# A macaron trunk on one core: the first modulation and the first products in two depth halves, with the tokens loaded between them

## What is computed

```python
mod   = silu(c)     @ w_ada + b_ada          # latent: s1, sc1, g1, s2, ...
mod_c = silu(c_ctx) @ w_ada + b_ada          # the same for the context
h = h + 0.5 * g1 * swiglu(modulate(rms_norm(h, g_ffn1), s1, sc1), w1_gate, w1_up, w1_down)
h = h + g2 * mixer(modulate(rms_norm(h, g_mix), s2, sc2))
h = h + 0.5 * g3 * swiglu(modulate(rms_norm(h, g_ffn2), s3, sc3), w2_gate, w2_up, w2_down)
# modulate(x, shift, scale) = x * (1 + scale) + shift;  out = rms_norm(h, g_final)
```

## Time and profile before

| | |
|---|---|
| runs | 2579.36, 2579.87, 2574.9 us |
| profiled execution | 2575.95 us, span 2574.2 us |
| TensorE matmul busy | 2502.8 us, 97% of the span |
| DVE / ACT / POOL busy | 1925.6 / 1156.1 / 737.0 us |
| first product of the first pair | 43.52 us |
| first product of the second pair | 66.08 us |
| DMA share, 10 to 40 us | 1.00 to 1.07 |

### The profile page before, as it was taken

The page is one execution under the profiler, slowest core; times in us unless marked ns, Lnnn a source line. Parts: engine busy times, 40 slices in busy tenths (PEclk is TensorE's granted clock), DMA queues, the critical chain, the costliest instruction groups (busy, mean ns, idle before and its releaser), DMA issues.

```text
span 2574.2 us, 40436 instructions
## 1 busy us (share of the span) xinstructions
PE 2502.8 (97%) x14986; PEld 2306.5 (90%) x14986; DVE 1925.6 (75%) x3245; ACT 1156.1 (45%) x2203; POOL 737.0 (29%) x654
## 2 busy tenths in 40 slices
PE   7999999999998999999999999999999999999998
PEld 4999999988888889999999899999998788899997
DVE  5788788766488588888755887888557596877776
ACT  5533433443387262432434624324344485544444
POOL 1321221224166231221132322212312264333332
PEclk8999999999999999999999999999999999999999
DMA  6344444214430124444312244453122431133332
GB/s 245 104 142 141 134 136 142 84 58 149 123 90 3 58 86 135 132 139 148 115 50 82 82 131 130 140 151 116 54 78 100 135 79 50 62 98 103 101 106 80
DMA packets 132003, 276.18 MB, mean 107 GB/s; under 512 B 15584, under 2 KB 35296, under 8 KB 130528
## 3 DMA queue, kind: packets, MB, share of 16 engines
q1 hardware_dynamic: 131808, 273.60, 34.4%
HBM read 260.43 MB, written 13.11 MB: 106 GB/s over the span
## 4 chain that ended last, share of the span: by engine, by line
PE 83%; DVE 10%; issue 3%; ACT 3%; POOL 1%; DMA 1%; SPq 0%; DVEq 0%; ACTq 0%; POOLq 0%
PE ring L1878 37%; PE ring L1983 23%; PE ring L1994 15%; DVE wlo L1473 3%; PE row L1814 2%; PE row L1798 1%; PE ring L1834 1%; ACT pth L1124 1%; DVE neg_max L1269 1%; PE ring L1773 1%; DVE xl L1584 1%; PE ring L1778 1%; DMA ada_early<-w_turned 1%; DVE rstd L1305 1%; DVE t_lat L1577 0%
## 5 line engine op out<-in xcount | busy, mean ns | idle before, releaser
L1473 DVE TENSOR_TENSOR wlo<-raw,whi 128x512 fp32r<-128x512 f32 (+2 forms) x672 | 506.4, 764 | 293.8 <-ACT whi L970 292.4
L970 ACT ACTIVATE whi<-raw 128x512 fp32r<-128x512 f32 (+2 forms) x672 | 399.2, 605 | 373.5 <-PE ring L1983 231.5
L1878 PE MATMUL ring<-xh,whi 128*128 128x384 f32 (+1 forms) x1280 | 413.2, 323 | 10.3 <-DVE rstd L1452 5.5
L1878 PE MATMUL ring<-xl,whi 128*128 128x384 f32 (+1 forms) x1280 | 411.4, 321 | 0.0
L1878 PE MATMUL ring<-xh,wlo 128*128 128x384 f32 (+1 forms) x1280 | 411.2, 321 | 0.0
L1878 PE MATMUL ring<-th,whi 128*128 128x384 f32 (+1 forms) x960 | 311.7, 325 | 2.4 <-DVE wlo L1473 1.6
L1878 PE MATMUL ring<-th,wlo 128*128 128x384 f32 (+1 forms) x960 | 310.8, 324 | 0.0
L1878 PE MATMUL ring<-tl,whi 128*128 128x384 f32 (+1 forms) x960 | 310.7, 324 | 0.0
L655 POOL TENSOR_TENSOR raw<-raw,s_two 128x512 f32<-128x512 f32 x80 | 123.3, 1541 | 624.8 <-DVE wlo L1473 580.9
L1480 DVE SCALAR_TENSOR_TENSOR ada_junk<-ada_tile,row 128x1024 bf16<-128x1024 f32 x256 | 301.2, 1213 | 0.0
L641 POOL TENSOR_TENSOR s_one<-raw 128x512 f32<-128x512 f32 x80 | 105.4, 1317 | 552.2 <-DMA raw<-w_gu 416.6
(11 more groups left out here) (217 smaller groups left out, 5484.8 us busy)
## 6 DMA issues: line engine op xcount, KB each, us to landing
raw<-w_gu SPq DMA_DIRECT2D x352, 256.0 KB, 3.1
ada_tile<-w_turned SPq DMA_DIRECT2D x130, 512.0 KB, 3.7
raw<-w_down SPq DMA_DIRECT2D x96, 256.0 KB, 3.5
raw<-w_down SPq DMA_DIRECT2D x64, 192.0 KB, 2.5
raw<-w_in SPq DMA_DIRECT2D x48, 256.0 KB, 3.4
raw<-w_down SPq DMA_DIRECT2D x64, 128.0 KB, 2.1
raw<-w_out SPq DMA_DIRECT2D x32, 256.0 KB, 8.1
ada_first<-w_first SPq DMA_DIRECT2D x4, 1536.0 KB, 13.3
```

Of the source, the lines that this page charges most:

```text
L970: act.activation(weights(q, 0, cols)[0], src[:, 0:cols], ACT.Copy).then_inc(whi_ready, 1)
L1473: dve.tensor_tensor(w_l, src[:, 0:cols], w_h.bitcast(F32), ALU.subtract).then_inc(wlo_ready, 1)
L1878: last = pe.matmul(out, w, x, start=(start and k == 0 and m == 0), stop=(k == HALF - 1 and m == 2), skip_group_check=not start)
```

## The change

- Loads: the conditioning rows come as one line on one partition (8 KB), ahead of unit 0. Four ones-by-line products on TensorE spread it over the partitions into PSUM; ACT's Silu reads it there and writes `cond_row`. Tokens and two weight pieces are loaded ahead of units 2 and 3 and tiles 14 and 15.
- Columns of `w_ada` are regrouped: units 0 and 1 with tiles 12 and 13 hold shift and scale of k = 0 to 3, units 2 and 3 with tiles 14 and 15 those of k = 4 to 7.
- The first norm and the first pair are written out on all engines, in two halves: x for k = 0 to 3, four k-steps for `ring[0]`, then units 2 and 3, then the second half. Context squares move behind `first_columns(1)`.
- Pieces of the first pair are ordered by half; the counts of `vec_ready`, `ada_biased` and `piece_used` are changed to go with that.

```diff
@@ -42,6 +42,8 @@
 HALF = KD // 2
+FIRST_COLS = (0, 1, 2, 3, 8, 9, 4, 5, 6, 7, 12, 13)
...
@@ -136,7 +138,8 @@
                         s["units"].append((i,))
                         s["pair"][i], s["raw_of"][i] = len(self.pieces), len(self.raws)
                         if i < PLAIN:
-                            for u, half in ((0, 0), (0, 1), (1, 0), (1, 1)):
+                            by_half = s["n"] == 0 and i == 0
+                            for u, half in ((0, 0), (1, 0), (0, 1), (1, 1)) if by_half else ((0, 0), (0, 1), (1, 0), (1, 1)):
                                 r = raw("gu", w, i, u, half)
                                 piece(r, frees=(r,))
                             continue
+        cond_line = sb("cond_line", [1, 2, D_MODEL], F32, at[0])
...
+        turned_mod = row[:, 1024:1024 + 2 * FIRST_TILES]
...
@@ -532,22 +538,22 @@
+            sp.dma_start(cond_line[:], c_rows[0:1]).then_inc(rows_loaded, 16)
             load_first(0)
-            sp.dma_start(cond_row[:], c_rows).then_inc(rows_loaded, 16)
             load_ada(FIRST_TILES)
             load_first(1)
             load_ada(FIRST_TILES + 1)
             for dst, src in ((gain, gains), (gain_final, g_final), (qkg, qk_gain), (sinks, sink), (chan, dft_chan)):
                 sp.dma_start(dst[:], src).then_inc(more_loaded, 16)
+            for i in range(HALF):
+                sp.dma_start(h[:, 2 * i:2 * i + 2, 0:SEQ], x_t[:, 2 * i:2 * i + 2]).then_inc(x_loaded[i], 16)
+            load_w(0, 2)
             load_first(2)
             load_early(FIRST_TILES + 2)
             load_first(3)
             load_early(FIRST_TILES + 3)
-            for i in range(HALF):
-                sp.dma_start(h[:, 2 * i:2 * i + 2, 0:SEQ], x_t[:, 2 * i:2 * i + 2]).then_inc(x_loaded[i], 16)
-            load_w(0, 2)
+            load_w(2, 2)
             sp.dma_start(h[:, :, SEQ:TOK], ctx_t).then_inc(ctx_loaded, 16)
-            load_w(2, 2)
             for s in stages:
                 layer, n = s["layer"], s["n"]
-                act.wait_ge(piece_used, s["pair"][i] + 2)
+                act.wait_ge(piece_used, s["pair"][i] + (3 if (n, i) == (0, 0) else 2))
...
-                if n == 0:
-                    act.wait_ge(ctx_loaded, 16)
-                    for d in range(KD):
-                        square_ctx(d)
...
+            def first_norm():
+                def scaled(p, d):
+                    a, b, _, c = halves(TOK)[p]
+                    act.wait_ge(t1_ready, KD * p + d + 1)
+                    t1 = t1_lat[:, d, a:b] if p == 0 else t1_ctx[:, d]
+                    act.activation(xh[:, d, a:b], t1, ACT.Identity, bias=modv[:, c, d:d + 1]).then_inc(mod_done, 1)
+                std(0, TOK, 0)
+                split_hi(1)
+                act.wait_ge(vec_ready, 2)
+                for d in range(HALF):
+                    scaled(0, d)
+                read_row(2)
+                split_hi(2, 2)
+                read_row(3)
+                act.wait_ge(vec_ready, 4)
+                act.wait_ge(ctx_loaded, 16)
+                for d in range(HALF, KD):
+                    square_ctx(2 * (d - HALF))
+                    square_ctx(2 * (d - HALF) + 1)
+                    scaled(0, d)
+                std(0, TOK, 1)
+                widen(0, TOK)
+                act.preload_act_table(ACT.Silu)
+                for d in range(KD):
+                    scaled(1, d)
+                    if d % 2 == 1:
+                        add_shift(0, TOK, 0, HALF + d // 2, 0)
...
@@ -1060,33 +1092,32 @@
-            act.wait_ge(rows_loaded, 16)
-            act.activation(cond_row[:], cond_row[:], ACT.Silu).then_inc(rows_ready, 1)
+            act.wait_ge(line_spread, 1)
+            for c in range(2):
+                last = act.activation(cond_row[:, c], cond_wide[:, c], ACT.Silu)
+            last.then_inc(rows_ready, 1)
             act.preload_act_table(ACT.Sqrt)
             def read_row(u):
                 act.wait_ge(ada_row_mm, u + 1)
                 if u >= 2:
                     act.wait_ge(first_turned, u - 1)
-                act.activation(ada_rows[:, u % 2], ring[0][0:2, u % 2 * SEQ:u % 2 * SEQ + ADA_COLS], ACT.Copy).then_inc(ada_row_read, 1)
+                act.activation(ada_rows[:, u % 2], ring[u % 2][0:2, SEQ:SEQ + ADA_COLS], ACT.Copy).then_inc(ada_row_read, 1)
             read_row(0)
-            read_row(1)
-            read_row(2)
             for d in range(KD):
                 act.wait_ge(x_loaded[d // 2], 16)
                 if d >= 2:
                     act.wait_ge(acc_first[0], d - 1)
                 act.activation(sq_lat[:, d % 2], h[:, d, 0:SEQ], ACT.Square).then_inc(sq_first[0], 1)
-                if d == HALF + 1:
-                    read_row(3)
-            split_hi(0, 2)
+            read_row(1)
+            split_hi(0)
             act.wait_ge(consts_ready, CONSTS)
             act.wait_ge(more_loaded, 16 * 5)
             for l in range(DEPTH):
                 last = act.activation(qkg[:, 2 * l:2 * l + 1], qkg[:, 2 * l:2 * l + 1], ACT.Copy, scale=SCALE)
             last.then_inc(qkg_ready, 1)
-            norm(0, TOK, 0, 0)
+            first_norm()
...
+                col = EARLY_COLS[i - FIRST_TILES] if i < FIRST_TILES + EARLY else i
...
-                    dve.wait_ge(ada_biased, 6 * layer + 2 * stage + 1)
+                    dve.wait_ge(ada_biased, 6 * layer + 2 * stage)
...
+            def first_columns(x):
+                dve.wait_ge(first_turned, 2 * x + 2)
+                wide = lambda a, b: bias_ada[:, a:b].rearrange("p (o n) -> p o n", o=1).broadcast_to([P, 2, b - a])
+                for m, col, many in ((6 * x, HALF * x, 4), (6 * x + 4, KD + HALF * x, 2)):
+                    dve.tensor_tensor(modv[:, :, col:col + many], turned_mod[:, 2 * m:2 * (m + many)].rearrange("p (m c) -> p c m", c=2),
+                                      wide(col, col + many), ALU.add).then_inc(first_ready, 1)
+                dve.wait_ge(ada_lat_done, 2 * x + 2)
+                dve.wait_ge(ada_ctx_done, 2 * x + 2)
+                a = EARLY_COLS[2 * x]
+                dve.tensor_tensor(modv[:, :, a:a + 2], modv[:, :, a:a + 2], wide(a, a + 2), ALU.add).then_inc(first_ready, 1)
+                dve.wait_ge(first_ready, 3 * x + 3)
+                ks = slice(HALF * x, HALF * x + HALF)
+                for c in range(2):
+                    dve.scalar_tensor_tensor(out=vec_scale[:, c, ks], in0=modv[:, c, KD + HALF * x:KD + HALF * x + HALF], scalar=1.0,
+                                             in1=gain[:, 0, ks], op0=ALU.add, op1=ALU.mult).then_inc(vec_ready, 1)
+                if x == 0:
+                    dve.tensor_scalar(shift_step[:], modv[:, :, 0:HALF], -1.0, None, ALU.mult).then_inc(step_ready, 1)
+                dve.wait_ge(vec_ready, 2 * x + 2)
+            def first_norm():
+                def scaled(p, ks):
+                    a, b, o, c = halves(TOK)[p]
+                    t1 = lambda d: t1_lat[:, d, a:b] if p == 0 else t1_ctx[:, d]
+                    for d in range(ks[0], ks[1] + 1):
+                        if d < ks[1]:
+                            dve.scalar_tensor_tensor(out=t1(d), in0=h[:, d, a:b], scalar=vec_scale[:, c, d:d + 1],
+                                                     in1=side[:, o:o + b - a], op0=ALU.mult, op1=ALU.mult).then_inc(t1_ready, 1)
+                        if (p, d) == (0, 2):
+                            split_lo(1)
+                        if d > ks[0]:
+                            e = d - 1
+                            dve.wait_ge(mod_done, KD * p + d)
+                            dve.scalar_tensor_tensor(out=xl[:, e, a:b], in0=t1(e), scalar=modv[:, c, e:e + 1],
+                                                     in1=xh[:, e, a:b].bitcast(F32), op0=ALU.add, op1=ALU.subtract).then_inc(x_ready, 1)
+                first_columns(0)
+                split_lo(0)
+                invert(0, TOK, 0)
+                dve.wait_ge(inv_done, 1)
+                for m in range(SEQ // P):
+                    last = dve.tensor_scalar(rstd[:, m * P:(m + 1) * P], ones[:], rms_inv[:, m:m + 1], None, ALU.mult)
+                last.then_inc(rwide[0], 1)
+                dve.wait_ge(rstd_spread[0], 1)
+                scaled(0, (0, HALF))
+                for i in range(FIRST_TILES + 2, FIRST_TILES + EARLY):
+                    dve.wait_ge(early_loaded[i % 2], 16)
+                    ada_columns(i, ada_early[:, i % 2], cond_row, ada_junk_first)
+                split_lo(2, 2)
+                first_columns(1)
+                scaled(0, (HALF, KD))
+                invert(0, TOK, 1)
+                dve.wait_ge(rstd_spread[1], 1)
+                scaled(1, (0, KD))
...
-            for i in range(FIRST_TILES + 2, FIRST_TILES + EARLY):
-                dve.wait_ge(early_loaded[i % 2], 16)
-                ada_columns(i, ada_early[:, i % 2], cond_row, ada_junk_first)
-            ada_bias(FIRST_TILES, FIRST_TILES + EARLY)
             for d in range(KD - 1):
```

(72 more changed lines are left out.)

13 lines of the change are left out of this document (7 added, 6 removed).

## The result

The changed kernel takes 2587.87 us (median; 2587.12 to 2590.54), beside 2577.7 us (2574.9 to 2579.87) for the kernel before on the same chip. The ratio is 1.004, 95% interval [1.0029, 1.0051]: slower by some 10 us. The forecast was 2585 (2577 to 2592), 7.0 us more than before. The profiled execution lies at 2587.18 us, its span is 11.2 us longer than before's.

A forecast was written before the change was run, and what follows sets the result against it. TensorE, busy 97% of 2574.2 us, bounds the kernel; its opening hangs on loads. First product comes 11.1 us earlier, but exposed units 2 and 3 and waits put the second pair 7.0 us later: 2585 us, range 2577 to 2592.

The forecast's parts named there:

- The sum: Start of the second pair of products: 73.1 us instead of 66.08, so +7.0 us on the whole kernel.
- The line: Four TensorE products spreading the conditioning line: taken as 5 us, from 4 to 9, delaying unit 0 by about 1 us.
- granted clock is 1.00 (2.4 GHz) to 36 us: Opening before the change: TensorE at full clock to 36 us, then at half, 0.97 again after 53.
- Units 0 and 1: First two weight units on TensorE: both through by 19.5 us, bounds 18.5 to 22.5.
- The sum of squares: Tokens' sum on TensorE, behind their landing: starts at 22.8 us instead of 34.98, takes 2.0 us at full clock.
- All this is covered by the wait for tokens; uncovered it costs at most 1 us: Line spread, units 0 and 1, Silu and tiles 12 and 13 hide behind token loads; at most 1 us otherwise.
- I carry a delay at 66.08 to the end one for one: From the second pair's start to the end: any delay there lengthens the kernel equally, the rest staying 2508.1 us.
- Everything waits on semaphores, not on clock time: After 66 us: weight loads wait for used pieces, POOL and DVE for x_ready, so delay carries through unchanged.
- Slow clock longer: Rival, units 2 and 3: half clock until unit 2 is through, +11.6 us; through half of unit 3, +14; chance 10%.
- Only half of the lateness: Rival, opening: first four steps at full clock following x, both new waits half covered, +3.5 us, about 2582; chance 16%.
- both waits: TensorE's new waits for x in the second half: 1.9 us before k=4, 0.9 us near the last context x.
- Dense opening: Rival: TensorE never late after 32.4 us, second pair at 61.9, -4.2 us, about 2574; chance 10%.

The follow-up runs named there:

- The dense run with the Silu first: Changed kernel with units 2 and 3 before the first k-steps, context sum behind the first half's, ScalarE's first Silu before four context shifts: 2577.97 us, ratio 1.0001.
- early-context run: Changed kernel with units 2 and 3 before the first k-steps, and the context's squares and sum ahead of all k-steps: 2580.61 us, ratio 1.0013.

## Why the prediction was right

**The path through the opening** held step by step. The forecast's times and those of the trace: first product 32.4 and 32.64; four k-steps to 38.3 and 38.6; units 2 and 3 until 49.2 and 49.03; modulation of the second half at 51.4 and 51.28; x for k=4 at 54.7 and 54.18; the context's sum at 59.5 and 59.49; first context x 64.5 and 64.51, last 70.0 and 70.02; second pair 73.1 and 72.97. That the differences were small is in part luck: two errors in the terms below hide each other. TensorE waited 1.49 and 1.03 us for `xl` (1.9 and 0.9 forecast) and 0.85 for the Silu, VectorE idled 4.98 before 51.28 (about 4). Clock at half from 28.3 to 38.5, where I had 25 to 40. The cause stands by two runs: with the units elsewhere or cut, 7.4 and 7.6 us come back.

**The number.** The sum gave +7.0 and the medians differ by 10.2. The profiled execution was to be at 2583.0 by that sum and was at 2587.18; the forecast of 2585 is nearer only because it was taken between 2583 and 2586.4.

**Terms that were mis-sized.** The line took 7.16 us, not 5: 0.9 for a record, twice the 0.44 that a unit's record gives at full clock (5.32 / 16 x 512/384), so all of it ran at the slow rate, although the view of the granted clock shows 1.00 in those microseconds. The forecast's "granted clock is 1.00 (2.4 GHz) to 36 us" took that view at its word. Units 0 and 1 ended at 23.1, not by 19.5, beyond the upper bound of 22.5. The sum of squares came at 24.32 and not at 22.8, because ScalarE's read of unit 0's row stands in front of its first square, and unit 0 was through on TensorE only at 18.0. "All this is covered by the wait for tokens; uncovered it costs at most 1 us" was wrong by half a microsecond. What hid this error is a second one: from this sum to the first product I counted 9.6 us and it took 8.3; the `rstd` of four columns took 0.88 (1.38 before), and `turn_first(1)` and the small instructions ran beside it.

**The step that failed** is "I carry a delay at 66.08 to the end one for one". The rest of the kernel was 2512.4 us long and not 2508.1, which by the forecast's own words shows it wrong in this part. Of these 4.3 us, 0.15 are the chain's 66.08 in place of 65.92, and 1.0 is the ruler: it is the last context x, whose delay of 8.1 goes on through POOL, and not the second pair with its 7.05. The forecast had the right number for it, 70.0 against 61.91, and then did not use it. The other 3.1 are the stretch at half clock near 578 us (1.5) and the part behind 2340 us (1.6). "Everything waits on semaphores, not on clock time" overlooked that the clock and the waits themselves differ between executions.

**The rivals.** *Slow clock longer* did not occur: the clock rose before the units, once the k-steps ran without gaps. *Only half of the lateness* did not occur: both waits came about uncovered. *Dense opening* did not occur either: it named 4.2 us, and against it that the second half can't be made before unit 3 is turned, which is what the trace shows. The dense run with the Silu first, another order of work with its first product at 43.53, got its second pair at 61.52 (61.9 in the rival), yet the x chain gave 3.1 us and the median nothing measurable. The rule of the Trainium skill that I weighed against the change ("TensorE: Matmul & The Clock Gate", section "HAM oscillation — how this bites in real kernels"), that a pause brings the slow clock back, agrees with the drop at 45 us in the early-context run, within a wait of 3.7 us. The drops at 55 us, behind a wait of 1.49 us, and near 570, behind one of 1.12, came after much shorter pauses than the waits for loads that the section describes. And the pause near 570 us shows that a pause of this size decides nothing for a single execution: it brought the drop in one trace of before and not in the other.

## What to carry to other kernels

When a start is moved forward, ask which work had been hidden in the wait that goes away, and put that work first in the queue, not behind the consumer of the early data; a first product 11 us earlier was worth nothing here, where the last input of the stage came 8 us later. Take as the ruler the chain that other engines hang on further down (here the last x, through VectorE and POOL), not the first instruction of the next loop. Before two spans are subtracted, compare the granted clock over the whole of both, and look at a second trace of the same kernel: here two traces of the kernel before differ by 5 us.
